# Turning the third and fourth quadrant of the up projection one slot later

## The reference

```
h = rmsnorm(x, mix_norm)
b_gate, c_gate, v = split(h @ conv_w_in, 3)
x = x + (b_gate * causal_conv3(c_gate * v, conv_w)) @ conv_w_out
h = rmsnorm(x, mlp_norm)
a = relu(h @ mlp_w1)          # 512 x 2048 @ 2048 x 8192   (the up projection)
x = x + (a * a) @ mlp_w2      # 512 x 8192 @ 8192 x 2048   (the down projection)
```

## Time and profile before

| | |
|---|---|
| median of three runs | 1984.58 us (1984.13 to 1985.06) |
| the profiled execution | 1984.31 us |
| its span, first to last instruction | 1982.6 us |
| mean granted TensorE clock | 1.000 |
| PE busy, share of the span | 99% |
| DVE busy | 75% |
| ACT busy | 43% |

### The profile page before, as it was taken

How to read it: one execution, slowest core, us unless ns; L and a number is a source line. 1 busy time by engine, 2 the same in 40 slices (tenths; PEclk the granted TensorE clock), 3 DMA queues, 4 the chain that set the end, 5 groups by cost and what they waited for, 6 DMA issues and landing times. The chain is left out here.

```text
span 1982.6 us, 23073 instructions
## 1 busy us (share of the span) xinstructions
PE 1958.6 (99%) x8778; PEld 1619.6 (82%) x8778; DVE 1485.2 (75%) x1496; ACT 860.8 (43%) x1002; POOL 75.3 (4%) x146
## 2 busy tenths in 40 slices
PE   8999999999999999999999999999999999999999
PEld 7888888888888788788888888888888888888887
DVE  6345353363453579999999999999889879878878
ACT  6222222222233455756657556575434433333332
POOL 0000000000000100101001011010000000000000
PEclk9999999999999999999999999999999999999999
DMA  5332223323233536757677576779989887887783
GB/s 192 106 106 88 103 85 106 106 85 106 85 106 106 199 124 235 284 219 293 262 295 301 207 306 263 280 314 350 361 339 354 326 329 298 316 331 293 279 330 126
DMA packets 98318, 445.93 MB, mean 225 GB/s; under 512 B 10800, under 2 KB 10800, under 8 KB 73776
## 3 DMA queue, kind: packets, MB, share of 16 engines
q1 hardware_dynamic: 78944, 375.42, 50.3%
q0 software_dynamic: 19136, 69.21, 8.6%
q10 hardware_dynamic: 144, 0.04, 0.0%
HBM read 371.24 MB, written 73.40 MB: 224 GB/s over the span
## 5 line engine op out<-in xcount | busy, mean ns | idle before, releaser
L1084 PE MATMUL pair<-ring,act 128*128 128x512 f32 x5376 | 1229.3, 390 | 0.2 <-DVE ring L799 0.2
L1084 PEld LDWEIGHTS pair<-ring,act 128*128 128x128 f32 x5376 | 1006.1, 188 | 209.2 <-DVE ring L799 0.9
L454 ACT ACTIVATE ring<-raw 128x1024 fp32r<-128x1024 f32 x448 | 474.9, 1061 | 595.3 <-PE pair L1084 431.5
L799 DVE TENSOR_TENSOR ring<-raw,ring 128x1024 fp32r<-128x1024 f32 x448 | 538.8, 1220 | 103.8 <-ACT ring L454 102.7
L599 DVE TENSOR_TENSOR w_lo<-w_raw,w_hi 128x512 fp32r<-128x512 f32 x256 | 175.5, 692 | 348.5 <-ACT w_hi L377 343.4
L377 ACT ACTIVATE w_hi<-w_raw 128x512 fp32r<-128x512 f32 x256 | 161.4, 631 | 474.0 <-PE pair L989 471.6
L793 DVE TENSOR_TENSOR raw<-raw 128x1024 f32<-128x1024 f32 x256 | 301.7, 1220 | 5.6
L989 PE MATMUL pair<-h_hi,w_lo 128*128 128x512 f32 x764 | 297.8, 390 | 0.0
L989 PE MATMUL pair<-h_hi,w_hi 128*128 128x512 f32 x764 | 297.2, 389 | 0.0
L989 PE MATMUL pair<-h_lo,w_hi 128*128 128x512 f32 x764 | 297.2, 389 | 0.0
L989 PEld LDWEIGHTS pair<-h_hi,w_lo 128*128 128x128 f32 x764 | 143.4, 188 | 30.7 <-issue 0.8
(11 more groups left out here) (89 smaller groups left out, 746.7 us busy)
## 6 DMA issues: line engine op xcount, KB each, us to landing
raw<-in_mlp SPq DMA_DIRECT2D x128, 1024.0 KB, 7.7
act<-spill SPq DMA_DIRECT2D x224, 512.0 KB, 6.4
w_raw<-in_weights SPq DMA_DIRECT2D x63, 1024.0 KB, 4.9
spill<-stage POOLq DMA_DIRECT2D x112, 512.0 KB, 8.6
act<-act_kept SPq DMA_DIRECT2D x84, 512.0 KB, 6.8
act_kept<-act POOLq DMA_DIRECT2D x12, 512.0 KB, 6.2
mixed<-turned POOLq DMA_DIRECT2D x16, 256.0 KB, 2.9
x<-mixed SPq DMA_DIRECT2D x8, 512.0 KB, 11.3
```

What stands on the lines that cost most here:

```text
L454: nc.scalar.activation(ring[g % RING][:, 0], raw[:, r, 2 * (s % 2):2 * (s % 2) + 2, :], ACT.Copy).then_inc(hi_ready, 1)
L799: nc.vector.tensor_tensor(ring[g % RING][:, 1], raw[:, RAW_OF[s // 2], 2 * (s % 2):2 * (s % 2) + 2, :], ring[g % RING][:, 0].bitcast(F32), ...
L1084: mm = nc.tensor.matmul(bank, stationary, moving, start=(opens and k == 0 and n == 0), stop=(closes and k == NT - 1 and n == 2))
```

## The change

The third and fourth quadrant are turned as slots 4 and 5 begin, in place of 3 and 4. The waits, the tiles and the order on the other engines stay as they are.

```
-                        if 2 <= v <= UP and v % 2 == 0 and s in (0, 2, 3, 4):
-                            turn_quad(v // 2 - 1, {0: 0, 2: 1, 3: 2, 4: 3}[s])
+                        if 2 <= v <= UP and v % 2 == 0 and s in (0, 2, 4, 5):
+                            turn_quad(v // 2 - 1, {0: 0, 2: 1, 4: 2, 5: 3}[s])
```

## The result

The changed kernel takes 1972.91 us (median of four runs, 1972.36 to 1973.64) against 1984.82 us (four runs, 1984.13 to 1985.41): a ratio of 0.9939, 95% interval 0.9928 to 0.9951. The forecast was 1973.0. The two profiled executions, 1984.31 and 1973.64 us, are only 10.7 apart: the new one came to its first turn 1.07 us later (795.81 against 794.74 us), ahead of anything that the change touches.

A forecast was written before the change was run, and what follows sets the result against it. PE, busy 99% of the span, was taken as the bound. Waits won of 2.37 us (first pair), 8.76 (six middle) and 0.52 (last) sum to 11.65, giving 1973.0 us; range 1972.0 to 1975.5.

The forecast's parts named there:

- The wait won: PE before the third turn: the whole wait goes, 1.46 us per middle pair, 2.37 first, 0.52 last, 11.65 together.
- The cause: Third turn on PE: it needs the PSUM pair back from ACT's second square, ready at 969.59, and PE is early.
- The fourth turn and L12: Fourth turn: third square ready 1.3 us ahead; L12 in slot 6: fourth square 1.1 us ahead, no wait.
- ACT's hold: ACT before the third square: it stands about 1.6 us instead of 0.30, holding the staged write and slot 7's split.
- DVE catches up: DVE before the next pair: 2.0 us of lag absorbed by 2.8 us of waits for splits, 0.8 left.
- D: DVE: delay of the low part of slot 7 behind ACT's hold, put at 0.55 us.
- rival 2: DVE becomes the bound: no lag regained, the second square stays late, time stays at 1984.6 us; chance 0.04.
- rival 3: ACT's hold behind the third square starves DVE, PE waits at the next third turn: about 1998 us; chance 0.03.
- The spills: POOL's spill behind the moved staged write: issued about 1.3 us later, hidden with the median landing of 8.6 us.

The follow-up runs named there:

- Run 3: Kernel before with the turns left in place and ACT's second square one slot earlier, in slot 4: 1974.09 us, 0.9947 of before.
- run 4: Kernel before with the change in the first of the eight pairs only: 1982.14 us, 0.9987 of before.
- Run 6: Changed kernel with five more activations on ACT in slot 7 of seven even visits, between third and fourth square: 1985.82 us, 1.0004 of the kernel before.
- run 2: Kernel before with third and fourth turn both at slot 4, one behind the other: 1984.02 us, 0.9997 of before.
- run 5: Changed kernel with two more activations on ACT in slot 7 of seven even visits, between third and fourth square: 1980.67 us, 0.9976 of the kernel before.
- run 8: Changed kernel with six more VectorE operations in slot 8 of seven even visits: 1989.26 us, 1.0022 of the kernel before.
- run 5 without the loads: Two extra activations as in run 5, without 42 loads of kept operands or their waits (visits 2 to 15): 1973.0 us, 0.9939 of the kernel before.
- run 9: Kernel before with six more VectorE operations in slot 8 of seven even visits: 1995.08 us, 1.0049 of the kernel before.

## Why the prediction was right

*The wait won.* 1.46 us per middle pair were forecast, 1.47 measured; 2.37 for the first pair, 2.38 measured (82.16 against 79.78 us to the next first turn). In all 11.65 were forecast and 11.91 measured by the medians. From the first pair's first turn to the end of the span the old trace takes 1982.6 - 794.74 = 1187.9 us, the new one 1971.8 - 795.81 = 1176.0: 11.9. Counting from start to start was right: the profile's own idle time, 10.3, is 1.6 us short of that. That the forecast came within 0.1 us of the median is luck: the four runs lie 1.3 us apart.

*The cause* is ACT's second square. Run 3 shows it from the other side, by moving the square and not the turns; run 4 shows that the pairs add up.

*The fourth turn and L12.* The fourth square was due 4.84 us after the third turn's start and came after 972.86 - 968.07 = 4.79; 1.1 us to spare were forecast and 1.18 measured (972.86 + 1.03 + 0.15 = 974.04, slot 6 at 972.49 + 2.73 = 975.22). Run 6 spends the margin and finds it where it should be, run 2 has the price of a turn that is too near.

*ACT's hold.* About 1.6 us forecast, 1.55 measured. That the staged write stands behind the third square though it needs only the second is the strict order of ACT's queue that the prediction took from the row; the row at 970.06 shows it again.

*DVE catches up.* D was put at 0.55 and is 0.50 (972.28 is 4.21 after the third turn's start; due, on the old clock, at 970.89 + 4.21 = 975.10 against 974.60). DVE's waits for splits were to fall from 2.8 to 0.8 a pair; the changed kernel's list for 958.8 to 1038 us:

```profile
DVE ring L799 <- ACT ring L454: 0.8, 1, 0.8
```

*What was wrong without hurting.* The prices of rivals 2 and 3 were built on the third turn as the place where DVE's lag would show, with 1.30 us of margin there (1.28 measured). Runs 5 and 8 show it first at L22's PSUM pair (1.0 us) and at the ring, and lag that a pair cannot regain adds up, so what counts is DVE's spare time in a pair, 1.9 us, and not the sum of margins. The spills were checked at one buffer only, the one whose write had moved; the edge lay at the sixth residual, where the changed kernel already waits 0.24 us in the third pair, and run 5 shows that 1.1 us more on ACT turns this into 7.8 us. It is not the length of the delay alone: 3.0 us more on ACT (run 6) leave a single such wait, of 1.5 us, and run 5 without the loads has none.

## What to carry to other kernels

Where a bound engine waits for a result by a fixed amount in each period, moving the consumer one step later wins the whole wait if the step is longer than the wait and the next user of the same buffer still has the chain (turn, square, turn, square) ahead of it: add that chain up on the in-order engine that carries it. Beside the margins ask what a helping engine has to spare in a period, since lag that is not regained there adds up. And every buffer that a DMA must drain before it is written again is such a margin too, with the longest landing and not the median.

## What the runs showed of the hardware

A wait of PE of 2.15 us was followed by some 3 to 4 us at the lower clock, at a cost of 1.6 us, in two of seven pairs of run 9; in the other five the same wait passed at full clock, and so did the first pair's 2.19 us of the kernel before. The Trainium skill ("TensorE: Matmul & The Clock Gate", section "What's actually happening") says that the gate is throttled by default and that activity releases it. The trace agrees as far as it goes: the granted clock was 1.00 through the pause and for the first 1.1 us behind it, 0.57 on the mean of the next 4 us, and 1.00 again with PE at work. Why two such waits were followed by the lower clock and the others not, no run here shows.

The landing of a 512 KB spill took 2.9 to 14.2 us in the up projection of the changed kernel, with a median of 8.4, so a buffer that is written again some ten us after its spill is issued is hidden by the median and not by the maximum.
